# Queries and forget gates of a gated linear layer: projected into feature-major form, with the weights stationary

## What is computed

```python
def hgrn2_layer(x, norm_w, w_in, lb, out_norm_w, w_out):
    h = rmsnorm(x, norm_w)              # x * rsqrt(mean(x^2) + EPS) * norm_w
    proj = h @ w_in                     # [256, 8192]: q | fz | i | gate, 2048 each
    ...                                 # 16 heads of 128 features
    log_f = jnp.logaddexp(jnp.log(lb), jnp.log1p(-lb) + jax.nn.log_sigmoid(fz))
    k = (1.0 - lb) * jax.nn.sigmoid(-fz)
    o = hgrn2_chunkwise(q, k, i, log_f) # linear attention with a decay per feature
    o = head_rmsnorm(o, out_norm_w)     # divides each head by its own root mean square
    o = o * jax.nn.silu(gate)
    return x + (o @ w_out)
```

## Time and profile before

| | |
|---|---|
| median of 3 runs | 1892.48 us (1892.23 to 1892.65) |
| time of the profiled execution | 1891.89 us |
| its span in the trace | 1890.1 us |
| TensorE busy | 1856.6 us, 98% of the span |
| VectorE busy | 1241.5 us, 66% |
| ScalarE busy | 982.9 us, 52% |
| DMA | 319.28 MB, mean 169 GB/s |
| granted TensorE clock, mean | 0.997 of full speed |

### The profile page before, as it was taken

One profiled execution on the slowest core, in us unless ns is written; L12 is line 12 of the kernel. 1 busy time (PEld: TensorE's weight loads), 2 busy tenths in 40 slices (PEclk: granted clock), 3 DMA queues, 4 the chain that ended last, 5 costly groups with the idle time before them and its releaser, 6 DMA issues.

```text
span 1890.1 us, 25046 instructions
## 1 busy us (share of the span) xinstructions
PE 1856.6 (98%) x9049; PEld 1559.8 (83%) x9049; DVE 1241.5 (66%) x1672; ACT 982.9 (52%) x1516; POOL 27.6 (1%) x106
## 2 busy tenths in 40 slices
PE   8999989999999999999999999999999999999999
PEld 7888878878888888887888888888878888878787
DVE  6566665687557755658777777777766555566664
ACT  4455564355456545536554454544435455566652
POOL 4000000000000000000000000000000000000000
PEclk9999999999999999999999999999999999999999
DMA  6665434468789877565545454544456566545453
GB/s 233 210 187 149 145 117 135 145 206 184 182 164 201 183 184 168 200 237 156 161 160 157 144 167 144 164 147 156 146 166 204 179 189 191 164 142 161 146 170 116
DMA packets 170207, 319.28 MB, mean 169 GB/s; under 512 B 16601, under 2 KB 20849, under 8 KB 169345
## 3 DMA queue, kind: packets, MB, share of 16 engines
q1 hardware_dynamic: 168992, 313.70, 56.7%
q10 hardware_dynamic: 576, 4.19, 0.5%
q0 software_dynamic: 544, 0.13, 0.0%
HBM read 315.88 MB, written 2.10 MB: 168 GB/s over the span
## 4 chain that ended last, share of the span: by engine, by line
PE 45%; DVE 2%; ACT 2%; issue 2%; ACTq 0%; DVEq 0%
PE acc L287 13%; PE acc L289 13%; PE acc L288 13%; PE ps L2640 3%; PE ps L538 1%; ACT whi L249 1%; DVE wlo L257 1%; PE ps L2624 0%; DVE arena L2014 0%; PE ps L381 0%; ACT arena L1440 0%; ACT arena L1376 0%; PE ps L2614 0%; PE ps L571 0%; PE ps L2721 0%
## 5 line engine op out<-in xcount | busy, mean ns | idle before, releaser
L257 DVE TENSOR_TENSOR wlo<-wraw,whi 128x1024 fp32r<-128x1024 f32 (+3 forms) x616 | 713.7, 1178 | 412.6 <-ACT whi L249 409.8
L249 ACT ACTIVATE whi<-wraw 128x1024 fp32r<-128x1024 f32 (+3 forms) x616 | 615.0, 1017 | 340.2 <-PE acc L289 334.4
L287 PE MATMUL acc<-whi,ta_hi 128*128 128x512 f32 x1664 | 659.4, 396 | 2.5 <-DVE wlo L257 2.3
L289 PE MATMUL acc<-whi,ta_lo 128*128 128x512 f32 x1664 | 648.6, 390 | 0.0
L288 PE MATMUL acc<-wlo,ta_hi 128*128 128x512 f32 x1664 | 647.9, 389 | 0.0
L287 PEld LDWEIGHTS acc<-whi,ta_hi 128*128 128x128 f32 x1664 | 312.6, 188 | 68.1 <-issue 3.4
L289 PEld LDWEIGHTS acc<-whi,ta_lo 128*128 128x128 f32 x1664 | 312.3, 188 | 66.6
L288 PEld LDWEIGHTS acc<-wlo,ta_hi 128*128 128x128 f32 x1664 | 312.8, 188 | 61.8
L287 PE MATMUL acc<-whi,tb_hi 128*128 128x512 f32 (+1 forms) x704 | 278.6, 396 | 8.2 <-DVE wlo L257 6.5
L289 PE MATMUL acc<-whi,tb_lo 128*128 128x512 f32 (+1 forms) x704 | 271.9, 386 | 0.0
L288 PE MATMUL acc<-wlo,tb_hi 128*128 128x512 f32 (+1 forms) x704 | 271.7, 386 | 0.0
(11 more groups left out here) (312 smaller groups left out, 1324.3 us busy)
## 6 DMA issues: line engine op xcount, KB each, us to landing
wraw<-in_ml_w_in SPq DMA_DIRECT2D x128, 512.0 KB, 6.1
wraw<-in_a_w_in SPq DMA_DIRECT2D x128, 512.0 KB, 4.0
wraw<-in_kv_w SPq DMA_DIRECT2D x64, 512.0 KB, 3.8
wraw<-in_b_w_in SPq DMA_DIRECT2D x64, 512.0 KB, 4.3
wraw<-in_mla_w_in SPq DMA_DIRECT2D x48, 512.0 KB, 5.3
wraw<-in_mla_w_out SPq DMA_DIRECT2D x32, 512.0 KB, 3.7
wraw<-in_ml_w_out SPq DMA_DIRECT2D x32, 512.0 KB, 4.6
wraw<-in_a_w_out SPq DMA_DIRECT2D x32, 512.0 KB, 4.4
```

The lines of the kernel that those rows point to most:

```text
L249: nc.scalar.activation(whi[:, n % SPLIT, :, 0:w], wraw[:, n % RAW, :, 0:w], ACT.Copy).then_inc(w_high, 1)
L257: nc.vector.tensor_tensor(wlo[:, n % SPLIT, :, 0:w], wraw[:, n % RAW, :, 0:w], whi[:, n % SPLIT, :, 0:w].bitcast(F32), ALU.subtract).then_ ...
L287: nc.tensor.matmul(o, xh, wh, start=first, stop=False)
L289: m = nc.tensor.matmul(o, xl, wh, start=False, stop=end)
```

## The change

For `l2` the forget gates in all four groups, and the queries in groups 1 to 3, are produced with the weights stationary: a block of 128x128 of `whi` or `wlo` is loaded, and 256 tokens of the activations stream past it. The result is feature-major in PSUM, two heads a bank. There is then nothing to transpose for them. The token factor lies along the free axis now. For forget gates DVE multiplies by a row `rrow`, the same in all partitions, which is made once in group 0 from a diagonal matrix (TensorE, `ones` times `rdiag2`, after unit 16). Queries are not scaled; the head norm adds EPS times the inverse square of the factor in place of EPS. The queries of group 0 keep the old product and their 8 transposes, are evacuated 3 units after their end, unscaled, and by themselves.

The whole forget tile is evacuated by DVE (two instructions), the whole query tile of groups 1 to 3 by ACT (two instructions). Waits on the evacuation of the tile before (`earlier_out`) are added to those and to ACT's evacuation of the values. `hn`, the scratch of ACT's squares, goes to `dT`.

```diff
+        def by_columns(name, k, it):
+            return name == "l2" and (k == FORGET_L2 or k == QUERY_L2 and not first(it))
...
+            if turned:                       # in products()
+                for j in range(KU):
+                    hi, lo, kk = src(k, q + j)
+                    for h in range(w // P):
+                        c = slice(h * P, (h + 1) * P)
+                        o = acc[:, tt % 2, h // 2, h % 2 * T:(h % 2 + 1) * T]
+                        wh, wl = whi[:, n % SPLIT, j, c], wlo[:, n % SPLIT, j, c]
+                        end = q + j == kt - 1
+                        nc.tensor.matmul(o, wh, hi[:, kk, :], start=q + j == 0 and h % 2 == 0, stop=False)
+                        nc.tensor.matmul(o, wl, hi[:, kk, :], start=False, stop=False)
+                        m = nc.tensor.matmul(o, wh, lo[:, kk, :], start=False, stop=end and h % 2 == 1)
+                m.then_inc(w_used, 1)
+                return
...
-        FIRST_L2 = 15
+        FIRST_L2 = 19
...
+        def queries_in(eng, g):
+            if first(g):
+                eng.wait_ge(l2["qT"], 1)
+            else:
+                landed(eng, "l2", QUERY_L2, g)
...
+                if name == "l2" and k == QUERY_L2 and not first(it):      # evac() on ACT
+                    tile_done(act, name, k, it)
+                    earlier_out(act, out_b1, name, k, it)
+                    for b, done in enumerate((out_b0, out_b1)):
+                        nc.scalar.activation(DST(name, k, b, it, act), result(name, k, b, P, it),
+                                             ACT.Copy).then_inc(done, 1)
+                    return
+                if name == "l2" and k == 2:
+                    earlier_out(act, out_b0, name, k, it)
...
                 def turned():                                             # ACT, group's "turn"
-                    act.wait_ge(l2["tq"], 1 + g)
-                    nc.scalar.activation(qT2.rearrange("p h t -> p (h t)"), ps2(0), ACT.Copy).then_inc(l2["qT"], 1)
+                    if first(g):
+                        act.wait_ge(l2["tq"], 1)
+                        nc.scalar.activation(qT2.rearrange("p h t -> p (h t)"), ps2(0),
+                                             ACT.Copy).then_inc(l2["qT"], 1)
...
+                if name == "l2" and k == FORGET_L2:                       # evac() on DVE
+                    tile_done(dve, name, k, it)
+                    if first(it):
+                        own.sync()
+                    earlier_out(dve, out_b0, name, k, it)
+                    earlier_out(dve, out_b1, name, k, it)
+                    for b, done in enumerate((out_b0, out_b1)):
+                        nc.vector.tensor_tensor(DST(name, k, b, it, dve), result(name, k, b, P, it),
+                                                rrow.unsqueeze(1).to_broadcast([P, 2, T]), ALU.mult).then_inc(done, 1)
+                    return
...
-                    f = ps2(2)                                            # DVE, "turn" and "decay"
-                    dve.wait_ge(l2["tf"], 1 + g)
+                    f = flat(fT2)
+                    landed(dve, "l2", FORGET_L2, g)
...
-                    nc.vector.tensor_scalar(sm[:, 32:40], sm[:, 32:40], 1.0 / HD, EPS, ALU.mult,
-                                            ALU.add).then_inc(l2["v"], 1)
+                    v = sm[:, 32:40].rearrange("p (b h) -> p b h", b=TB)
+                    nc.vector.scalar_tensor_tensor(v, v, 1.0 / HD, nrm[:, :, 0:1].to_broadcast([P, TB, 4]), ALU.mult,
+                                                   ALU.add).then_inc(l2["v"], 1)
...
+            def token_scales():                                           # DVE
+                dve.wait_ge(nrm_a, 6)
+                for b in range(TB):
+                    nc.vector.tensor_scalar(rdiag2[:, b * P:(b + 1) * P], ident[:], nrm[:, b, 2:3], None,
+                                            ALU.mult).then_inc(l2["r_dg"], 1)
+                own.mark(nc.vector.tensor_scalar(nrm[:, :, 0], nrm[:, :, 3], EPS / D, EPS * EPS, ALU.mult, ALU.add))
+            def token_row():
+                dve.wait_ge(l2["r_row"], 1)
+                own.mark(nc.vector.tensor_copy(rrow, ps[:, 2, 0:T]))
...
             for p in range(SPLIT + 1, length("l2")):
                 step(dve, low, evac, "l2", p)
...
+                if p == 16:
+                    token_scales()
+                if p == 18:
+                    token_row()
...
                 def turned():                                             # TensorE
-                    landed(pe, "l2", 1, g)
-                    for w, bank in ((qw2, 0), (fw2, 2)):
+                    if first(g):
+                        landed(pe, "l2", QUERY_L2, g)
                         for h in range(4):
                             for b in range(TB):
-                                m = nc.tensor.transpose(ps2(bank)[:, h * T + b * P:h * T + (b + 1) * P],
-                                                        w[:, b, h * P:(h + 1) * P], ident[:])
-                        m.then_inc(l2["tq" if bank == 0 else "tf"], 1)
+                                m = nc.tensor.transpose(ps2(0)[:, h * T + b * P:h * T + (b + 1) * P],
+                                                        qw2[:, b, h * P:(h + 1) * P], ident[:])
+                        m.then_inc(l2["tq"], 1)
...
                 products(pe, "l2", p, in_src)
+                if p == 16:
+                    pe.wait_ge(l2["r_dg"], 2)
+                    pe.wait_ge(tr_lo, turn.n)
+                    nc.tensor.matmul(ps[:, 2, 0:T], ones[:, 0:P], rdiag2, start=True, stop=True).then_inc(l2["r_row"], 1)
                 l2_side(0, p)
```

More of the change, by code:

```diff
@@ L265, in products @@
             w, kt, nu, n, tt = tiles[k][4], tiles[k][1], units(tiles), UNIT[name] + p, TILE[name] + k
+            turned = by_columns(name, k, it)
+            assert not turned or blocks == (0, 1)
             if q == 0 and tt >= 2:
@@ L320, in tile_done, with result @@
             eng.wait_ge(w_used, UNIT[name] + ends(name)[k] + 1 + units(tiles) * it)
-        def result(name, k, b, rows):
+        def result(name, k, b, rows, it=0):
+            if by_columns(name, k, it):
+                return acc[:, (TILE[name] + k) % 2, b, :].rearrange("p (h t) -> p h t", t=T)
             w, bank = PHD[name][1][k][4], (TILE[name] + k) % 2
@@ L361, in step @@
             for k, e in enumerate(ends(name)):
-                if p == (FIRST_L2 if name == "l2" and k == 0 and first(it) else e + LAG):
+                if p == (FIRST_L2 if name == "l2" and k == FORGET_L2 and first(it) else e + LAG):
                     evac(name, k, it)
@@ L749, in build @@
         A = Carve()
-        qw2, fw2, vw2, gw2 = [A(TB, COLS) for _ in range(4)]
+        vw2, gw2 = [A(TB, COLS) for _ in range(2)]
         G4 = 4 * T
-        qT2, kT2, bT2 = A(4, T), A(4, T), A(4, T)
+        fT2 = A(4, T)
+        rrow = A(T)
+        kT2, bT2 = A(4, T), A(4, T)
+        qw2, qT2 = A(TB, COLS), A(4, T)
         aT = A(8, P)
@@ L756, in build @@
         qx = A(2, 2 * T)
-        l2 = sems(2, "tq tf qT nf lf kx kt ge gs dg at df ee op lv sel pv sq ss v rs on og ogp tmp hi lo")
+        rdiag2 = qx[:, 0, 0:T]
+        l2 = sems(2, "r_dg r_row tq qT nf lf kx kt ge gs dg at df ee op lv sel pv sq ss v rs on og ogp tmp hi lo")
         def dst_l2(name, k, b, it):
-            return (qw2, fw2, vw2, gw2)[k][:, b, :]
+            if k == QUERY_L2:
+                return qw2[:, b, :] if first(it) else qT2[:, 2 * b:2 * b + 2, :]
+            if k == FORGET_L2:
+                return fT2[:, 2 * b:2 * b + 2, :]
+            return (vw2, gw2)[k - 2][:, b, :]
         def free_l2(eng, name, k, it):
[L769 to L772, removed]
+            if k == QUERY_L2 or k == 2:
                 if not first(it):
                     eng.wait_ge(l2["pv"], it)
+            elif k == FORGET_L2:
+                if first(it):
+                    eng.wait_ge(tr_src, 4)
             else:
@@ L983, in evac @@
                     return
+                if name == "l2" and k == FORGET_L2:
+                    return
                 FREE(act, name, k, it)
-                if name in SCALED:
+                if name == "l2" and k == QUERY_L2 and not first(it):
[7 more added lines that the diff above has]
+                    earlier_out(act, out_b0, name, k, it)
+                if name in SCALED and not (name == "l2" and k == QUERY_L2):
                     tile_done(act, name, k, it)
@@ L1265, in stream_scale @@
                 act.wait_ge(tr_src, 2 + b + 1)
-                own.then(nc.scalar.activation(hn[:, b, :], x_res[:, b, :], ACT.Square, accum_out=nrm[:, b, 3:4]))
+                own.then(nc.scalar.activation(dT.rearrange("p a n -> p (a n)"), x_res[:, b, :], ACT.Square,
+                                              accum_out=nrm[:, b, 3:4]))
                 own.then(nc.scalar.activation(nrm[:, b, 1:2], nrm[:, b, 3:4], ACT.Ln, scale=1.0 / D, bias=eps_col))
```

16 lines of the change are left out of this document (9 added, 7 removed).

## The result

The changed kernel takes 1894.61 us (median of 20 runs, 1892.34 to 1895.6) beside 1892.05 us (20 runs, 1890.14 to 1893.75) for the kernel before: ratio 1.0012, interval 1.0006 to 1.0017. It is 1.1 to 3.2 us slower. Forecast were 1887.9 us, 4.6 us less, in a range of 1886.6 to 1893.4; both the direction and the range were missed.

What follows compares the result with a forecast made beforehand. TensorE, busy 98% of the span, was taken as the bound. Transposes -3 x 1.75, waits -1.05, group 0 +1.7 and the rest 0 gave -4.6 us, so 1887.9 us, range 1886.6 to 1893.4.

Steps and rivals of the forecast that it cites:

- the price of the turned products: Seven query and forget tiles: 1344 matmuls of 256 columns at 0.1134 us each, costing nothing; upper bound 0.120, +8.9 us.
- the excess belongs to the full-width load: Rival, chance 0.12: full load and equally long fp32r stream disturb each other, 0.120 per new matmul, +8.9 us, 1896.8 total.
- a few nanoseconds on each matmul: Rival, chance 0.28: jitter or a fixed part on all 1344, 0.1155 to 0.118 each, costing 2.8 to 6.2 us.
- The direct sample of the earlier trace: One 256-column fp32r matmul on 128x128 took 0.12 us; standing alone, it may hold a cost of changing kind.
- 48 transposes, groups 1 to 3: TensorE in groups 1 to 3 loses 16 transposes each, 1.75 us a group, 5.25 us in all.
- wait, groups 1 to 3: TensorE's wait for keys ahead of the diagonal products shrinks from 0.55 to 0.2 us a group, gaining 1.05 in three.
- first diagonal products, group 0: Group 0's diagonal products on TensorE start 1.4 to 1.9 us later than before; 1.7 taken.
- the round trip: Group 0: TensorE makes the token-scale row after unit 16, VectorE copies it before evacuating; diagonal products 1.7 us later.
- The turn of VectorE: Group 0: VectorE's work on the forget tile after evacuation and low part starts 1.8 to 1.9 us late.
- wait by the head norm: ScalarE's second query evacuation precedes the previous group's head norm; 2.4 us cover some 0.6, so no cost; otherwise 1.8 us.
- the added waits between evacuations: Waits on evacuations that are a tile or half a tile old; claimed to cost nothing.
- the other signs: L2614 transposes absent in groups 1 to 3, 8 in group 0; diagonal products of groups 2 and 3 each 2.1 us closer.

Runs made afterwards that it cites:

- split kernel: Kernel before, nothing turned, 512-column matmuls of the same seven query and forget tiles each cut into two of 256: 1899.99 us, ratio 1.0042.
- exchanged transposes: Kernel before with one line changed, TensorE transposing forget gates first and queries after: 1890.33 us, ratio 0.9989; timed again 1889.38 us, ratio 0.9987.
- the early row: Changed kernel with the row of token scales made two units earlier and the first forget tile evacuated at step 18: 1891.99 us, ratio 1.0002.

## Why the prediction was wrong, point by point

The step that failed is the price of the turned products: "I take 0.1134, a cost of nothing". It is 0.1200, 6.6 ns more, and the split kernel, with nothing turned, gives the cost of it as +7.94 us. The mechanism stood among the rivals, with a chance of 0.12 ("the excess belongs to the full-width load"), at 0.120 and +8.9 us. The other rival, a few nanoseconds on each matmul (0.28), had 0.1155 to 0.118 and is out by the pace. I weighed the right one low by a wrong reading: that half the columns took half the time with a narrow load was taken as proof that nothing is fixed. The trace of before held the rows that speak against it, and I left them out: fp32r streams of 384 columns with a full-width load, in the first layer.

```profile
113.56 0.33 PE L289 MATMUL acc<-whi,tb_lo 128*128 128x384 f32 x1
...
115.64 0.33 PE L289 MATMUL acc<-whi,tb_lo 128*128 128x384 f32 x1
```

12 distances in 2.08 us are 0.1733. With 0.2267 for 512, 128 columns more cost 0.0534, and so 256 columns fewer than 512 leave 0.2267 - 0.1068 = 0.1199. A straight line through two shapes with the same load gives the measured pace within 0.1 ns: 13.3 ns are fixed and 0.417 ns belong to a column. What in the engine takes the 13.3 ns is open; the runs with narrower loads and with mixed lengths show that it is not one fixed price of a load. The direct sample of the earlier trace rows, 0.12, also read right; I explained it away.

Term by term, in us:

| term | predicted | measured |
|---|---|---|
| 1344 turned matmuls | 0 (rival +8.9) | +7.94, split kernel |
| 48 transposes, groups 1 to 3 | -5.25 | -5.16, 3 x 1.72 from the lengths of a group |
| wait, groups 1 to 3 | -1.05 | -2.15, 3 x 0.72 by the exchanged transposes |
| first diagonal products, group 0 | +1.7 | +1.02 |
| sum | -4.6 | +1.65 by these terms, +1.67 in the stretch |

For groups 1 to 3 the closing of the sum proves little, since 1.72 is what the changed kernel's own group leaves over. What counts there is that it comes out beside the 1.75 read ahead from the transposes themselves: they were on the path, as the prediction had it.

Group 0: the diagonal products are 928.33 - 866.89 = 61.44 us behind the start of the stretch, before 59.14; of the 2.30, 1.28 is the pace, as in the split kernel. This leaves 1.02 for the round trip, where 1.7 was forecast. The turn of VectorE starts here:

```profile
914.87 0.69 DVE L2070 TENSOR_SCALAR arena<-arena 128x1024 f32<-128x1024 f32 x1
```

That is 47.98 behind the start of the stretch, beside 45.15 before, so 1.55 late without the pace, where 1.8 to 1.9 was forecast. From the turn to the diagonal products are 13.46 us in place of 13.99, a gain of 0.53 where 0.4 was the most expected. The cause and the path were right, as the early row confirms. The place was right in part: the prediction wanted 2 to 2.6 us of wait at the diagonal products and none at a low part, and the trace has 1.46 there and 0.39 at the low part of unit 20.

The wait in groups 1 to 3 went, all of it, by the turn starting 2.34 us behind the tile (forecast some 2.5); its worth was 1.1 too low, in part since some of it was thought to stay and in part for the marks that a wait leaves behind. No wait by the head norm, by the added waits between evacuations or by the low parts of groups 1 to 3 shows in the list above.

Of the other signs, the queries' 8 transposes of group 0 are there and those of groups 1 to 3 are gone. But the diagonal products come only 0.19 us less behind those of the group before, and not 2.1: the pace takes 2.23 of it back.

All terms but the pace are -6.3 us together and were forecast as -4.6. That these errors ran against the large one is luck: without them the miss would be 1.7 us larger. The balance of a turned tile is what turned the sign: 8 transposes are worth 0.86 us, 192 matmuls cost 1.1 to 1.3.

The rule of the Trainium skill, "TensorE: Matmul & The Clock Gate", section "Back-to-back issue gap", gives 2.5 ns for each matmul in its formula for the isolated gap. The trace agrees that there is a fixed part and not with its size for fp32r: 13.3 ns here. The 672 matmuls more would cost 1.7 us by the rule, an estimate, and cost 7.9 by the trace.

## What to carry to other kernels

Before a stream is cut or turned, take the pace from at least two lengths with the same width of load, and see what a line through them leaves at zero columns. On an engine that is busy 98% of the time an order that starts the longest side chain first can be worth more than removing the work: exchanging two sets of transposes gave 2.9 us, and dropping 56 of 64 of them gave 0.45 us at best, with the early row, since the turned products took back the rest. When a change of a few microseconds sits in one stretch, the distance of two starts in the trace resolves it to hundredths. When a change lets a chain start earlier, see also whether the engine that waits for the chain's end arrives earlier by as much; only the difference of the two is gained.

## What was not expected of the hardware

The pace of fp32r streams with a full 128x128 load lies on one line at 256, 384 and 512 columns (0.1200, 0.1733, 0.2267 us), with some 13 ns for each matmul beside its columns. With narrower loads the pace of one and the same shape settles at one of several values, 0.1138 and 0.1165 us for 64 wide, and so does a pair of mixed lengths, at 0.347 and 0.355; why stays open.

The granted clock of TensorE fell in some executions and not in others, at more than one place ahead of the layer. The kernel with exchanged transposes, traced twice, reached the start of the stretch at 868.65 and at 865.28 us. Two stretches of the first trace, then of the second (us, busy by engine, clock, DMA):

```profile
235.00:255.00 20.00, 17.24 (x92) 15.43 (x91) 13.71 (x28) 12.40 (x23) 0.00 (x0) 0.91 0.35 108
855.00:870.00 15.00, 12.59 (x62) 10.16 (x61) 12.36 (x22) 12.58 (x28) 0.00 (x0) 0.89 0.33 105
```

```profile
235.00:255.00 20.00, 17.23 (x98) 15.12 (x97) 14.36 (x32) 13.81 (x25) 0.00 (x0) 1.00 0.39 123
855.00:870.00 15.00, 12.92 (x67) 10.49 (x66) 13.72 (x24) 14.19 (x32) 0.00 (x0) 1.00 0.37 116
```

0.91 and 0.89 are means over the two levels of 2.4 and 1.2 GHz. From these rows the clock lost is 0.09 x 20 + 0.11 x 15 = 3.45 us, an estimate, beside the 3.37 between the two starts. The kernel before had 0.91 and 1.00 in these two places and the changed one 1.00 and 0.89, so they reach the layer at nearly the same time, 867.06 and 866.89. What makes the clock fall in one execution and not in another no run shows. So a single trace's span carries some 3 us that say nothing of the change, which is another reason to read the stretch.
